# Masks added in half-height tiles beside the scores, from folded copies of the constant masks

## The chip, the cores and the metric

The kernel runs on one core of a Trainium2 chip. The metric is the device time of one launch in microseconds (us); each kernel is run several times and the median counts. The engines are TensorE (PE, with its weight loads listed apart as PEld), VectorE (DVE), ScalarE (ACT), GpSimd (POOL) and SyncE (SP), which issues all DMAs of this kernel in the order of its program.

## The reference

Two transformer layers with four kinds of attention are followed by a second block with a gated delta rule and a dilated attention. The sequence has 512 tokens and a head 64 channels. What matters here is how scores are masked; shortened:

```
# group a: causal, head width 96      # group d: causal, plus forget gates
s = einsum('bqhd,bkhd->bhqk', q_blk, k) * scale
if log_f_cum is not None:
    s = s + (cum[t] - cum[s])                       # group d only
s = where(key_pos <= qpos, s, -inf)
p = softmax(s)
# group b: sliding window of 128 keys, two key blocks, with a sink logit per head
mask = (kpos >= 0) & (kpos <= qpos) & (qpos - kpos < SWA_WINDOW)
s = where(mask, s, -inf)
# group c: each query keeps its top 128 keys by an indexer; for the first block plain causal
# second block, dilated attention, three groups: window of 2 blocks, causal, residue classes
scores = where((dist >= 0) & (dist <= n_back) & (kpos >= 0), scores, -inf)
```

## The kernel before, in words

A job is one head and one block of 128 queries: its scores against up to 512 keys, softmax, transposition of the probabilities and the product with the values. A layer has 64 jobs in 32 pairs; `layer_jobs` lists them by group in the order a, b, d, c (`JOB_ORDER`), so pairs 0 to 7 are group a, 8 to 15 group b, 16 to 23 group d, 24 to 31 group c. The dilated attention of the second block has 48 jobs in 24 pairs: 0 to 7 with the window mask, 8 to 15 causal, 16 to 23 residues. The two jobs of a pair are two heads: one has its channels in partitions 0 to 63, the other in 64 to 127 (`r` is 0 or 64). Their score products use those 64 rows of the array only, and the two stand side by side in it.

`attention` writes one program for each engine. PE's loop over p does the scores of pair p (with the mask), then, if p is odd and at least 5, the values of two earlier pairs, then, from p = 3, the transposes of pair p - 3. The scores of pair p go to four PSUM banks in turn, so they wait (`powered`) for the exponentials of pair p - 2. A mask is added by TensorE too: a bf16 identity of 128 rows times a bf16 mask of 128 rows, accumulated on the scores, one such product a job (L708). DVE then takes the row maximum (L773) and the shift (L779 or L782), ACT the exponential (L863), DVE the reciprocal (L806), POOL the scaling (L904), PE transposes (L722), ACT (in the dilated attention also DVE) copies, PE multiplies by the values (L741). On DVE steps of the key selection (L1992, L1993) stand between the pairs. Every float32 product comes as two passes, each with a weight load.

SP's program is one queue in the order of the blocks in the code. `Weights.send` (L141) issues a weight transfer when a slot of the ring is free, which it learns from the semaphore `split` that DVE's low part (L161) counts up. Before the change `attention` has no SP program; the transfers of the part before it are the last thing that SP issues until the part behind it.

Of the kernel before, what the change touches and what calls it, by code (L numbers as in the profile page):

```python
# [32 lines left out]
P = 128  # L33
S = 512
# [209 lines left out]
def opening(part, nc, sb, psum, weights, x, operand, small, a):  # L244
# [5 lines left out]
    ident_half = sb("ident_half", [P, P], BF16)  # L250
    causal_half = sb("causal_half", [P, P], BF16)
    window_half = sb("window_half", [P, 2 * P], BF16)
# [141 lines left out]
    return ((ident, ones, causal, (ident_half, causal_half, window_half), gate_forms, eps),  # L394
# [258 lines left out]

class Job:
# [5 lines left out]
    def __init__(self, scores, width, mask, scale, values, sink=None, sinks=None):  # L660
        self.scores, self.width, self.mask, self.scale = scores, width, mask, scale
        self.values, self.sink, self.sinks = values, sink, sinks
# [6 lines left out]
def attention(block, psum, jobs, stores, ident, ident_half, probs, probs_t, stats, sems, besides=None, ready={},  # L669
              freed=None, turns_ready=(), values_ready=(), held=None, fill=None):  # L670
# [9 lines left out]
     dve_own, besides_done, sink_shifted, sink_powered) = sems  # L680
# [13 lines left out]
    def _(pe):  # L694
        def scores(p):
# [201 lines left out]
    def _(pool):  # L897
# [3 lines left out]
        for j in range(n):  # L901
# [6 lines left out]
                  "dve_own besides_done sink_shifted sink_powered")  # L908
# [266 lines left out]
def layers(nc, psum, x, operand, weights, consts, vectors, plans, small, besides_last, a, first, opened, begin):  # L1175

    ident, ones, causal, (ident_half, causal_half, window), gate_forms, eps = consts
    all_gains, all_sinks, all_forget_bias = vectors
    table_rows = nc.inline_tensor(tables(), name="position_tables")
    for l, (_, n_out, n_down) in enumerate(plans):  # L1180
# [9 lines left out]
        with opened if l == 0 else ExitStack() as whole:  # L1190
            layer = first if l == 0 else whole.enter_context(part(nc))
            with ExitStack() as mix:
# [20 lines left out]
                with ExitStack() as ctx:  # L1213
                    jobs = layer_jobs(turned, values, gates, kept, causal_half, window, sinks)
# [7 lines left out]
                    probs_t = sb("probs_t", [P, 4, S], ctx)  # L1222
                    sb("kept_free", [P, T * LATENT_W + TABLE_W - 4 * S], ctx)
# [4 lines left out]
                              output.fill(stored_low, (powered, n_jobs)))  # L1228
# [768 lines left out]
def layer_jobs(turned, values, gates, chosen, causal, window, sinks):  # L1997

    jobs = []
    for group in JOB_ORDER:  # L2000
        for pair in range(2):
            for t, h in itertools.product(range(T), (2 * pair, 2 * pair + 1)):
# [4 lines left out]
                sink = both = None  # L2007
                scale = 64 ** -0.5
                if group == "a":
                    scale = 96 ** -0.5  # L2010
                    scores = [(turned[0:MLA_DIM, QA + h, q], turned[0:MLA_DIM, KA + h, 0:w])]
                    v0 = V_MLA + 64 * h
                    v = [values[:, b, v0:v0 + 64] for b in blocks]
                elif group == "b":
                    blocks = list(range(max(t - 1, 0), t + 1))
                    k0 = blocks[0] * P
                    mask = window[:, 2 * P - len(blocks) * P:2 * P]
                    sink, both = sinks[:, h:h + 1], sinks[:, 2 * pair:2 * pair + 2]
# [3 lines left out]
                elif group == "c":  # L2022
                    if t:
                        mask = chosen[:, t - 1, 0:w]
# [1445 lines left out]
```

## Time and profile before

| | us |
|---|---|
| median of 3 runs (lowest, highest) | 2065.27 (2065.0, 2066.26) |
| profiled execution, its own time | 2066.51 |
| profiled execution, span from first to last instruction | 2064.8 |

| engine | busy us | share of the span |
|---|---|---|
| PE | 1990.1 | 96% |
| PEld | 1610.8 | 78% |
| DVE | 1115.5 | 54% |
| ACT | 832.9 | 40% |
| POOL | 361.3 | 17% |

The shares are means over stages that differ. Nearly all of PE's time is in the dense products (L182 to L184); the stages that the change touches are three: the attention of layer 0 (about 170 to 255 us in the span), that of layer 1 (about 820 to 915 us) and the dilated attention (1878 to 1922 us). In these the clock of TensorE and the waits between the engines are to be read by stretches, not from the totals. In the page's line of the clock each digit is the granted share in tenths of full speed.

### The profile page before, as it was taken

The page shows a single profiled execution, that of the slowest core. Times are in us where ns is not written, and L with a number is a line of the kernel's source. Part 1 is how long each engine was busy: PE and PEld are TensorE (multiplying, and loading weights), DVE is VectorE, ACT ScalarE, POOL GpSimd, SP SyncE. Part 2 cuts the span into 40 slices and gives each one's busy share as a digit, 9 for nine tenths or more (in the row PEclk, how much of TensorE's full clock was granted, in tenths as well). Part 3 has the DMA queues.
Part 4 walks back from the last instruction along what each step waited for, and adds up shares of the span by engine and source line. Part 5 has one row for each costly group of instructions (what it writes and reads, how often), then busy time and mean ns, then how long its engine had stood idle before and what let it go on. Part 6 is the DMA issues. An engine that isn't in the chain of part 4 may idle for free. (4 is left out here: it accounts for less than half of the span.)

```text
span 2064.8 us, 27438 instructions
## 1 busy us (share of the span) xinstructions
PE 1990.1 (96%) x10488; PEld 1610.8 (78%) x10488; DVE 1115.5 (54%) x2037; ACT 832.9 (40%) x1736; POOL 361.3 (17%) x345
## 2 busy tenths in 40 slices
PE   8999999999999999999999999799999999999997
PEld 7776588888887877568888888688787987886786
DVE  5788644423434489835643543579775331525555
ACT  4445633322423244744321332453443334534532
POOL 1336700000000153740000000003031320004300
PEclk9999999999999999999999999999999999999999
DMA  6321023323333442013533433223225222341232
GB/s 192 96 79 52 1 73 110 103 92 92 99 105 79 115 107 75 12 48 107 201 136 107 168 115 110 89 77 92 83 70 146 80 71 95 93 143 42 82 123 82
DMA packets 177523, 198.27 MB, mean 96 GB/s; under 512 B 38755, under 2 KB 140786, under 8 KB 176882
## 3 DMA queue, kind: packets, MB, share of 16 engines
q1 hardware_dynamic: 177394, 196.53, 30.8%
q8 instruction: 84, 1.38, 0.3%
q14 instruction: 45, 0.37, 0.1%
HBM read 180.74 MB, written 11.55 MB: 93 GB/s over the span
## 5 line engine op out<-in xcount | busy, mean ns | idle before, releaser
L161 DVE TENSOR_TENSOR weight_pairs<-weight_ring,weight_pairs 128x1024 fp32r<-128x1024 f32 (+4 forms) x293 | 355.3, 1215 | 399.4 <-ACT weight_pairs L152 398.2
L182 PE MATMUL psum<-operand,weight_pairs 128*128 128x512 f32 x1320 | 527.3, 399 | 11.6 <-PEq L230 8.6
L184 PE MATMUL psum<-operand,weight_pairs 128*128 128x512 f32 x1320 | 517.3, 392 | 0.0
L183 PE MATMUL psum<-operand,weight_pairs 128*128 128x512 f32 x1320 | 517.2, 392 | 0.0
L152 ACT ACTIVATE weight_pairs<-weight_ring 128x1024 fp32r<-128x1024 f32 (+4 forms) x293 | 303.4, 1038 | 524.9 <-PE psum L184 510.4
L182 PEld LDWEIGHTS psum<-operand,weight_pairs 128*128 128x128 f32 x1320 | 249.3, 189 | 71.4 <-issue 19.4
L184 PEld LDWEIGHTS psum<-operand,weight_pairs 128*128 128x128 f32 x1320 | 248.8, 188 | 53.8
L183 PEld LDWEIGHTS psum<-operand,weight_pairs 128*128 128x128 f32 x1320 | 249.4, 189 | 50.8 <-issue 1.0
L904 POOL TENSOR_SCALAR probs<-probs,stats 128x128 f32<-128x128 f32 (+3 forms) x176 | 162.4, 940 | 228.6 <-DVE stats L806 227.3
L182 PE MATMUL psum<-weight_pairs,hidden 128*128 128x512 f32 x512 | 200.6, 392 | 0.0
L183 PE MATMUL psum<-weight_pairs,hidden 128*128 128x512 f32 x512 | 199.9, 391 | 0.0
L184 PE MATMUL psum<-weight_pairs,hidden 128*128 128x512 f32 x512 | 199.9, 390 | 0.0
L1351 DVE TENSOR_TENSOR mlp_work<-mlp_work 128x512 f32<-128x512 f32 x64 | 44.0, 688 | 175.3 <-ACT mlp_work L1334 175.3
L182 PE MATMUL psum<-weight_pairs,operand 128*128 128x512 f32 (+3 forms) x320 | 115.7, 362 | 5.3 <-DVE weight_pairs L161 3.7
L182 PEld LDWEIGHTS psum<-weight_pairs,hidden 128*128 128x128 f32 x512 | 96.6, 189 | 20.3 <-issue 0.2
L184 PEld LDWEIGHTS psum<-weight_pairs,hidden 128*128 128x128 f32 x512 | 96.5, 189 | 20.1
L183 PEld LDWEIGHTS psum<-weight_pairs,hidden 128*128 128x128 f32 x512 | 96.4, 188 | 20.2 <-issue 0.2
L183 PE MATMUL psum<-weight_pairs,operand 128*128 128x512 f32 (+3 forms) x320 | 112.1, 350 | 0.0
L184 PE MATMUL psum<-weight_pairs,operand 128*128 128x512 f32 (+3 forms) x320 | 112.1, 350 | 0.0
L863 ACT ACTIVATE probs<-psum,stats 128x128 f32<-128x128 f32 (+3 forms) x176 | 82.8, 482 | 28.2 <-DVE stats L779 26.1
L1334 ACT ACTIVATE mlp_work<-psum 128x512 f32<-128x512 f32 x64 | 37.6, 594 | 137.9 <-PE psum L184 137.9
L773 DVE TENSOR_REDUCE stats<-psum 128x1 f32<-128x128 f32 (+3 forms) x176 | 66.3, 418 | 29.6 <-PE psum L708 29.1
(433 smaller groups left out, 2760.8 us busy)
## 6 DMA issues: line engine op xcount, KB each, us to landing
weight_ring<-in_w_in_dram SPq DMA_DIRECT2D x100, 512.0 KB, 3.7
weight_ring<-in_w_up_dram SPq DMA_DIRECT2D x64, 512.0 KB, 3.7
weight_ring<-in_w_down_dram SPq DMA_DIRECT2D x64, 512.0 KB, 3.6
weight_ring<-in_w_out_dram SPq DMA_DIRECT2D x24, 512.0 KB, 3.5
ada_rows<-in_ada_w_dram SPq DMA_DIRECT2D x24, 512.0 KB, 4.6
spilled<-v_t SPq DMA_DIRECT2D x22, 256.0 KB, 4.3
weight_ring<-in_w_in_dram SPq DMA_DIRECT2D x20, 256.0 KB, 2.9
weight_ring<-in_w_proj_a_dram SPq DMA_DIRECT2D x8, 512.0 KB, 3.4
```

The lines of the kernel that those rows point to most:

```text
L152: act.activation(self.pairs[:, i % SPLIT_RING, 0, 0:n], self.buf[:, i % RING, 0:n], ACT.Copy).then_inc(self.rounded, 1)
L161: dve.tensor_tensor(self.pairs[:, i % SPLIT_RING, 1, 0:n], self.buf[:, i % RING, 0:n], self.pairs[:, i % SPLIT_RING, 0, 0:n].bitcast(F32), ...
L182: pe.matmul(out, lhs[0], rhs[0], start=start, stop=False)
L183: pe.matmul(out, lhs[0], rhs[1], start=False, stop=False)
L184: return pe.matmul(out, lhs[1], rhs[0], start=False, stop=stop)
L773: dve.tensor_reduce(stats[:, 4, j:j + 1], psum[:, j % SB, 0:jobs[j].width], AX_X, ALU.max).then_inc(found, 1)
L863: act.activation(probs[:, j % PB, 0:job.width], psum[:, j % SB, 0:job.width], ACT.Exp, bias=stats[:, 0, j:j + 1], scale=job.scale, accum_o ...
L904: pool.tensor_scalar(rows, rows, stats[:, 2, j:j + 1], None, ALU.mult).then_inc(normed, 1)
L1334: act.activation(self.relu[:, g % B, :], self.psum[:, g % 8, :], ACT.Relu).then_inc(self.rectified, 1)
L1351: dve.tensor_tensor(self.square[:, f % B, :], self.relu[:, f % B, :], self.relu[:, f % B, :], ALU.mult).then_inc(self.squared, 1)
```

## The change

The three bf16 constants (identity, causal mask, window mask) become one tile, `halves`. Each attention gets an SP program. It first waits for `turns_ready` (in the layers; the list is empty in the dilated attention) and then copies the constants from SBUF to SBUF into a tile `folds` of two halves: half i has rows 64i to 64i + 63 of a constant, once in partitions 0 to 63 and once in 64 to 127. That takes four copies a source: one source in a layer (4 copies of 64 x 512 in bf16), three in the dilated attention (8 copies of 64 x 128, 4 of 64 x 256). They land in memory that the stage before has freed; in the dilated attention that is the old float32 `causal`. PE waits for all of them (`masks_folded`) at the first pair that uses them: pair 8 in a layer, pair 0 in the dilated attention.

A job of groups b and d, of c in its first query block, and of the dilated groups 0 and 1 now adds its mask by two products of 64 rows each, in the same rows as its scores. Group a, the chosen masks of group c and the residue masks stay as they were. In group d the gate products (2 rows of the array) come ahead of the score products instead of behind them.

```diff
@@ attention
+    folds, sources = folded
+    by_rows = [p for p in range(len(jobs) // 2) if jobs[2 * p].mask_rows is not None]
+
+    @block.sync
+    def _(sp):
+        for sem, count_needed in turns_ready:
+            sp.wait_ge(sem, count_needed)
+        at = 0
+        for source in sources:
+            width = source.shape[1]
+            for r in (0, P // 2):
+                for i in range(2):
+                    sp.dma_start(folds[r:r + P // 2, i, at:at + width],
+                                 source[i * P // 2:(i + 1) * P // 2, :]).then_inc(masks_folded, 16)
+            at += width
@@ attention, PE, scores(p)
+            if p == by_rows[0]:
+                pe.wait_ge(masks_folded, 16 * 4 * len(sources))
+            if p in by_rows:
+                for i in range(2):
+                    for j in pair:
+                        shifted_ident, rows_of_mask = jobs[j].mask_rows[i]
+                        first = jobs[j].width - rows_of_mask.shape[1]
+                        mm = pe.matmul(psum[:, j % SB, first:jobs[j].width], shifted_ident, rows_of_mask, start=False,
+                                       stop=(i == 1))
+                        if i == 1:
+                            mm.then_inc(scored, 1)
+                return
@@ layer_jobs, group d
-                    scores = [(turned[r:r + 64, DQ + h // 2, q], turned[r:r + 64, DK + h // 2, 0:w]),
-                              (gates[32 * h:32 * h + 2, 0, q], gates[32 * h:32 * h + 2, 1, 0:w])]
+                    scores = [(gates[32 * h:32 * h + 2, 0, q], gates[32 * h:32 * h + 2, 1, 0:w]),
+                              (turned[r:r + 64, DQ + h // 2, q], turned[r:r + 64, DK + h // 2, 0:w])]
@@ new function; folds has identity at columns 0 to P, causal from P, window from 2 P
+def mask_in_halves(folds, r, at, width):
+    side = slice(r, r + P // 2)
+    return [(folds[side, i, 0:P], folds[side, i, at:at + width]) for i in range(2)]
@@ dilated attention
+                halves = mask_in_halves(folds, r, (4 * P - w, P)[g], w) if g < 2 else None
+                  folded=(folds, (ident_half[:], causal[:], window_incl[:])))
```

On PE the rows of layer 0, group b, read so before the change (`turned_qk` are scores, `ident,probs` transposes, `probs_t,values` the values):

```order
L705 MATMUL psum<-turned_qk 128x256 x2
L708 MATMUL psum<-window_half,ident_half 128x256 x2
L741 MATMUL psum<-probs_t,values 64x128 x6
L722 MATMUL psum<-ident,probs 128x128 x6
L705 MATMUL psum<-turned_qk 128x256 x2
L708 MATMUL psum<-window_half,ident_half 128x256 x2
L722 MATMUL psum<-ident,probs 128x128 x8
```

and after it:

```order
L727 MATMUL psum<-turned_qk 128x256 x2
L735 MATMUL psum<-folded_masks 128x256 x4
L775 MATMUL psum<-probs_t,values 64x128 x6
L756 MATMUL psum<-ident,probs 128x128 x6
L727 MATMUL psum<-turned_qk 128x256 x2
L735 MATMUL psum<-folded_masks 128x256 x4
L756 MATMUL psum<-ident,probs 128x128 x8
```

The places are the same; the two mask products of a pair have become four of half height.

On SP, at the way from the product stage of the second block to the dilated attention, the queue reads before:

```order
L141 DMA weight_ring<-in_w_proj_a_dram 128x4x256 x2
L141 DMA weight_ring<-in_w_in_dram 128x4x256 x6
L3194 UNCONDITIONAL_BRANCH
L3197 DMA qk<-spilled 128x6x512
L141 DMA weight_ring<-in_w_in_dram 128x4x256 x2
```

and after:

```order
L141 DMA weight_ring<-in_w_proj_a_dram 128x4x256 x2
L141 DMA weight_ring<-in_w_in_dram 128x4x256 x6
L690 UNCONDITIONAL_BRANCH
L699 DMA causal<-halves 64x128 x8
L699 DMA causal<-window_incl_half 64x256 x4
L3236 UNCONDITIONAL_BRANCH
L3239 DMA qk<-spilled 128x6x512
```

The twelve copies stand behind the last of six weight transfers and so can't be issued ahead of it. In a layer the four copies stand in the same way behind the sixth transfer of the output weights (`in_w_out`); here, of the program after, with the awaited semaphores:

```order
L141 DMA weight_ring<-in_w_out_dram 128x2x512 [waits weights_split] x6
L690 UNCONDITIONAL_BRANCH [waits front_0_copied_bk]
L699 DMA folded_masks<-halves 64x512 [waits front_0_tokens_stored]
L699 DMA folded_masks<-halves 64x512 x3
L1134 UNCONDITIONAL_BRANCH
L141 DMA weight_ring<-in_w_out_dram 128x2x512 [waits weights_split]
```

The weight transfer that used to follow the branch at once now stands behind the four copies and their wait.

## Rows read from the trace of the kernel before

**Rows 1.** The page: busy time, and the chain that ended last.
```profile
PE 1990.1 (96%) x10488; PEld 1610.8 (78%) x10488; DVE 1115.5 (54%) x2037; ACT 832.9 (40%) x1736; POOL 361.3 (17%) x345
PE 13%; ACT 1%; DVE 1%; issue 1%; ACTq 0%
```

**Rows 2.** Stretches: length, busy us per engine; clock, DMA share, GB/s.
```profile
1882.40:1889.00 6.60, 6.24 (x27) 3.58 (x28) 4.31 (x22) 4.39 (x19) 4.69 (x6) 0.50 0.00 0
...
1889.30:1900.00 10.70, 10.52 (x102) 7.05 (x100) 7.35 (x36) 7.19 (x30) 9.57 (x13) 1.00 0.01 2
190.00:200.00 10.00, 8.22 (x80) 5.41 (x78) 9.03 (x35) 7.37 (x26) 7.72 (x7) 1.00 0.15 52
```

**Rows 3.** Timeline of PE, group b of layer 0: start, length, instruction.
```profile
205.11 0.41 PE L705 MATMUL psum<-turned_qk 64*128 64x256 f32 x2
205.45 0.39 PE L708 MATMUL psum<-window_half,ident_half 128*128 128x256 bf16 x2
...
205.77 0.88 PE L741 MATMUL psum<-probs_t,values 128*64 128x128 f32 x12
206.58 0.66 PE L722 MATMUL psum<-ident,probs 128*128 128x128 f32 x4
...
207.48 0.38 PE L705 MATMUL psum<-turned_qk 64*128 64x256 f32 x2
207.80 0.39 PE L708 MATMUL psum<-window_half,ident_half 128*128 128x256 bf16 x2
208.03 0.60 PE L722 MATMUL psum<-ident,probs 128*128 128x128 f32 x4
```

**Rows 4.** The same for its weight loads.
```profile
207.27 0.19 PEld L705 LDWEIGHTS psum<-turned_qk 64*128 64x128 f32 x2
207.79 0.11 PEld L708 LDWEIGHTS psum<-window_half,ident_half 128*128 128x128 bf16 x2 [0.33 <-issue]
207.92 0.47 PEld L722 LDWEIGHTS psum<-ident,probs 128*128 128x128 f32 x4
```

**Rows 5.** Timeline of SP: last transfer before each of the three attention stages.
```profile
1875.35 0.37 SPq L141 DMA_DIRECT2D weight_ring<-in_w_in_dram  x1
...
190.15 0.37 SPq L141 DMA_DIRECT2D weight_ring<-in_w_out_dram  x1
...
836.01 0.37 SPq L141 DMA_DIRECT2D weight_ring<-in_w_out_dram  x1
```

**Rows 6.** Copies from SBUF to SBUF in the trace: timeline, and issues with us to landing.
```profile
99.44 4.98 SPq L1625 DMA_DIRECT2D turned_qk_first<-turned_qk  x8
...
turned_qk_first<-turned_qk SPq DMA_DIRECT2D x56, 64.0 KB, 2.0
```

**Rows 7.** Timeline at the start of the dilated attention, PE and DVE.
```profile
1878.70 0.29 PE L708 MATMUL psum<-window_incl_half,ident_half 128*128 128x128 bf16 x2
1881.41 0.70 PE L705 MATMUL psum<-qk,q_dilated 64*128 64x256 f32 x4 [2.42 <-DVE v_tok L2867]
...
1881.28 0.48 DVE L773 TENSOR_REDUCE stats<-psum 128x1 f32<-128x128 f32 x2
```

**Rows 8.** Timeline around the first pair of group b, layer 0, then layer 1.
```profile
192.95 0.28 PE L708 MATMUL psum<-window_half,ident_half 128*128 128x128 bf16 x2
...
193.88 0.44 PE L722 MATMUL psum<-ident,probs 128*128 128x128 f32 x2 [0.42 <-POOL probs L904]
194.78 0.70 PE L705 MATMUL psum<-turned_qk 64*128 64x256 f32 x4 [0.46 <-ACT probs L863]
...
199.73 0.66 PE L722 MATMUL psum<-ident,probs 128*128 128x128 f32 x4 [0.90 <-POOL probs L904]
...
193.93 0.47 DVE L773 TENSOR_REDUCE stats<-psum 128x1 f32<-128x128 f32 x2
...
839.20 0.28 PE L708 MATMUL psum<-window_half,ident_half 128*128 128x128 bf16 x2
```

**Rows 9.** Timeline of PE, dilated attention, clock granted at 0.50.
```profile
1884.50 1.22 PE L705 MATMUL psum<-qk,q_dilated 64*128 64x256 f32 x4
```

More of the change, by code:

```diff
@@ L651, in finish_act, with __init__ @@
             self.high(act, T - 1)
+def mask_in_halves(folds, r, at, width):
+    side = slice(r, r + P // 2)
+    return [(folds[side, i, 0:P], folds[side, i, at:at + width]) for i in range(2)]
 class Job:
-    def __init__(self, scores, width, mask, scale, values, sink=None, sinks=None):
+    def __init__(self, scores, width, mask, scale, values, sink=None, sinks=None, mask_rows=None):
+        self.mask_rows = mask_rows
         self.scores, self.width, self.mask, self.scale = scores, width, mask, scale
@@ L1213, in layers @@
                 with ExitStack() as ctx:
-                    jobs = layer_jobs(turned, values, gates, kept, causal_half, window, sinks)
+                    probs_t = sb("probs_t", [P, 4, S], ctx)
+                    folds = sb("folded_masks", [P, 2, 4 * P], ctx, BF16)
+                    jobs = layer_jobs(turned, values, gates, kept, causal_half, window, sinks, folds)
                     n_jobs = len(jobs)
@@ L1994, in select_keys, with layer_jobs @@
     return (T - 1) * per_tile, step
-def layer_jobs(turned, values, gates, chosen, causal, window, sinks):
+def layer_jobs(turned, values, gates, chosen, causal, window, sinks, folds):
     jobs = []
@@ L2017, in layer_jobs @@
                     mask = window[:, 2 * P - len(blocks) * P:2 * P]
+                    halves = mask_in_halves(folds, r, 4 * P - len(blocks) * P, len(blocks) * P)
                     sink, both = sinks[:, h:h + 1], sinks[:, 2 * pair:2 * pair + 2]
@@ L2028, in layer_jobs @@
                 else:
-                    scores = [(turned[r:r + 64, DQ + h // 2, q], turned[r:r + 64, DK + h // 2, 0:w]),
-                              (gates[32 * h:32 * h + 2, 0, q], gates[32 * h:32 * h + 2, 1, 0:w])]
+                    scores = [(gates[32 * h:32 * h + 2, 0, q], gates[32 * h:32 * h + 2, 1, 0:w]),
+                              (turned[r:r + 64, DQ + h // 2, q], turned[r:r + 64, DK + h // 2, 0:w])]
                     v0 = tok("dv") + 64 * h
                     v = [values[:, b, v0:v0 + 64] for b in blocks]
-                jobs.append(Job(scores, w - k0, mask, scale, v, sink, both))
+                jobs.append(Job(scores, w - k0, mask, scale, v, sink, both, halves))
     return jobs
@@ L3164, in dilated_attention @@
                 mask = (window_incl[:, 2 * P - w:2 * P], causal[:], residues[:])[g]
+                halves = mask_in_halves(folds, r, (4 * P - w, P)[g], w) if g < 2 else None
                 jobs.append(Job([(q[r:r + 64, c, b * P:(b + 1) * P], k[r:r + 64, c, keys])], w, mask, 64 ** -0.5,
-                                [v[:, kb, c * P + r:c * P + r + 64] for kb in blocks]))
+                                [v[:, kb, c * P + r:c * P + r + 64] for kb in blocks], mask_rows=halves))
     stores = [(permuted(y[:, c, :], c // 2), lambda bank, g=c // 2: in_order(bank, g), None)
```

32 lines of the change are left out of this document (17 added, 15 removed).

## The prediction

> **What bounds the kernel now.** I read the page first. PE is busy 96% of the span, mostly with dense products, and the chain that ended last lies on PE [rows 1]; a cost or a gain on PE's path is passed on to the end, if no wait takes it up on the way. So the question is what PE's path does in the three attention stages. I read them by stretches: in group b of layer 0 PE is busy 8.22 of 10 us and DVE 9.03, so there PE waits for the others; at the start of the dilated attention the clock is granted at 0.50 of full (1.2 GHz), and a little later it is full (2.4 GHz) and PE is busy 10.52 of 10.70 us [rows 2]. Then the timeline of PE pair by pair, and last SP's, since the change makes PE wait for copies that SP issues [rows 5].
>
> **What a mask costs now.** Passes of 128 columns in float32 follow each other at 0.11 us: four transposes take 0.60 us of which the last is 0.27 long, so 0.33 for three steps [rows 3]. A pass of 256 columns is thus 0.21 us. The second pass of the scores starts at 207.48 and has streamed by 207.70 (estimate, 207.48 + 0.21, rounded). The weights of the mask load at 207.79 [rows 4]: 0.10 us in which PE goes over from half-height tiles to the full array. The two mask products take 0.12 each, and the transposes behind them, in the same full-array form, start at 208.03 with their weights loaded under the mask, at 207.92 [rows 3, 4]. From the end of the scores to the transposes: 0.33 us. Where the values follow (odd pairs), the scores' last pass starts at 205.14 (205.11, and 0.03 more, by which the row's 0.41 is longer than the 0.38 of one pass), has streamed by 205.36, and the values begin at 205.77, to which 0.06 of open loading comes (twelve in pairs: 0.88 less 0.27 is 0.61, five steps of 0.11 are 0.55): 0.47 us, with two changes of form of 0.10 in it.
>
> **What it costs after.** The four half-height products of a pair stand two and two side by side, as the scores do: the two steps take 0.21 us together for 256 columns (a bf16 column needs half of float32's time: 0.12 with its load against 0.21). There is no change of form ahead of them, one behind.
> - Even pair, transposes follow: 0.21 + 0.10 + 0.06 (the transposes' first weights, no longer loaded under a mask; as at 206.58, where four take 0.66 instead of 0.60) = 0.37 against 0.33: 0.04 us, with the skew of the two tiles 0.05 longer.
> - Odd pair, values follow: 0.21 + 0.10 + 0.06 = 0.37 against 0.47: 0.10 us shorter.
> With masks of 128 columns both sides shrink alike and the differences stay. In group d the gate products ahead instead of behind change the order of the forms, not their number: before scores, gates, mask, after gates, scores with mask; the same sums hold.
> Count: a layer has 8 odd and 10 even pairs (b and d, and two first blocks of c), the dilated attention 6 odd and 7 even from pair 3 on. Odd: 22 x 0.10 = 2.2 us less; even: 27 x 0.05 = 1.35 more. Pairs 0 to 2 of the dilated attention lose both changes of form, at the slow clock; there PE mostly waits for ACT, so I take 0.3 less. Sum of PE's path: 1.1 us less. In group b PE waits for DVE and ACT anyway [rows 2, 8], so part of it is not seen: bounds 0 and, if every one of the 52 pairs gained 0.10, 5.2 us less. I take 1.0, nearest to the rows.
>
> A rule speaks against even this. The Trainium skill (TensorE: Matmul & The Clock Gate, Part 3, The mechanism) says that a weight load overlaps with products in flight only when it goes to another row group. The second mask product of a job goes to the row group of the first. The trace does not agree: the second weights of the scores load at 207.27, in the same 64 rows in which the first pass streams until 207.48 [rows 3, 4]. By the rule the loads would stand open; what that costs is the second rival.
>
> **The copies, the part that costs.** No such copy of bf16 constants is in the trace, but the float32 copies from SBUF to SBUF are its nearest kin: eight issues take 4.98 us, 0.62 each, and a copy lands 2.0 us after its issue [rows 6]. The other end is the 0.37 us that SP takes for a weight transfer [rows 5]. I take 0.62, since both ends of these copies are in SBUF too.
> - Dilated attention: SP's last weight transfer is issued at 1875.35 [rows 5] and can't go earlier, since it waits for a ring slot. The first copy then starts at about 1875.85, the twelfth 11 x 0.62 = 6.8 later at 1882.7, and lands at 1884.7. PE wants the masks at 1878.70 [rows 7]. Not all of these 6 us count: DVE is busy with the stage before and takes the first maximum at 1881.28, and PE's second pair waits until 1881.41 [rows 7]. After: masks at 1884.7, about 0.4 to the first maximum (two steps and the latency of a matmul at the slow clock): 1885.1. Cost 3.8 us. PE's idle time at the slow clock moves with it: I expect the clock back at full some 3.4 us later than the 1889 of before, which keeps the stretch at 1.2 GHz about as long, at no further price.
> - Layer 0: last transfer at 190.15, copies at 190.65, 191.3, 191.9 and 192.5, landed at 194.5; PE wants them at 192.95: a stall of 1.55 us. Behind the wait stand the transposes of pair 5 and all that follows. PE has waits of its own at 193.88 (0.42), 194.78 (0.46) and 199.73 (0.90, for POOL, which works off pairs scored before) [rows 8]; they take up the stall on PE. DVE's maximum of pair 8 moves from 193.93 to 194.9, and DVE is 90% busy [rows 2], so a part stays: I take 0.3.
> - Layer 1: last transfer at 836.01, landed at 840.4, wanted at 839.20 [rows 5, 8]: a stall of 1.2 us, and 0.3 stays, by the same pattern.
> The waits of SP cost nothing else: the next transfer on the queue is issued at the end of each stage. `turns_ready` is reached before the first transposes, long before pair 8. The memory traffic of the copies is small beside one weight transfer.
>
> **Sum.** 3.8 + 0.3 + 0.3 - 1.0 = 3.4, rounded to 3.5 us more. The profiled execution took 2066.5 us (span 2064.8 and 1.7 around it) and would take 2070.0; it lies 1.2 above the median, so the median goes from 2065.3 to 2068.8: 0.17% more. A measurement of this kernel can tell about 0.2%, 4.1 us, from no change, so this is no change by that bound, but near it.
>
> **Rivals.**
> - The waits are paid in full (slower). In both layers the stall is passed on by DVE, whose slack is a tenth of its time: 1.55 + 1.2 instead of 0.6, 2.1 more; and PE, idle for 6 us at the dilated attention instead of 2.4, gets one more stretch at 1.2 GHz, in which the scores of a pair take 1.22 instead of 0.70 us [rows 7, 9]: about 0.7 for two pairs with their masks. 3.5 + 2.8 = 6.3: 2071.6. It decides from the point at which PE's waits behind the stall stay as long as they were (0.42, 0.46 and 0.90 in layer 0). For it: DVE's 9.03 of 10. Against: POOL's queue is long enough that PE waits for it at 199.73 in any case.
> - The loads of the second mask products stand open, since each goes to the rows of a product in flight (slower). The mask's load at 207.79 is 0.01 ahead of its product; a float32 load shows 0.06, two tiles 0.12 [rows 3, 4]. I take the middle, 0.06 for 52 pairs, 3.1 us: 2071.9. Against it: the second weights of the scores, loaded at 207.27 under a running pass. This is the skill's rule named above, as a mechanism of this kernel.
> - The copies come cheap: issued at 0.37 each, the twelfth starts at 1879.9 and lands at 1881.9. Then the first maximum comes 1.0 instead of 3.8 later, and the stalls in the layers shrink by 0.75 each: 3.5 - 2.8 - 0.4 = 0.3: 2065.6, the same.
> - The changes of form are worth more than the count says (faster): the copies cheap, and every pair 0.10 shorter because the maximum also starts sooner: 1.4 for the waits less 5.2: 2061.5. Against it: for 256 columns the first job's mask ends no sooner than before (0.10 + 0.12 against 0.11 + 0.11), and DVE begins with it.
>
> **How the numbers follow.** Forecast 0.50, waits in full 0.22, loads open 0.05, copies cheap 0.16, faster 0.07. The forecast's own spread is 1.5 us either way (0.37 to 0.62 an issue on one side, the layers' waits on the other), so a third of it lies over 4.1 us. Slower: 0.17 + 0.19 + 0.04 = 0.40; faster 0.06, as the last rival may also end within the bound; the same 0.54. The range goes from the cheap copies, 2065.6, to the dear waits, 2071.6 and half a us for the phase of the clock: 2072.1.
>
> **What would show it.** In the profile after: twelve copies on SP 0.6 apart from 1875.8 on; PE's mask of the first dilated pair at 1884.7 and the first maximum 0.4 behind it; the mask of pair 8 at 194.5 and 840.4 with the later waits shorter; from the end of an odd pair's scores to the values 0.10 less, to an even pair's transposes 0.05 more; four mask products in two steps of 0.11. Wrong would be the forecast if the copies are issued at another pace, if the two half-height products of a step don't run side by side, or if the whole stage of a layer is over 1 us longer.

## The result, and the profile after

| | us |
|---|---|
| kernel after, median of 4 runs (lowest, highest) | 2073.89 (2072.03, 2079.86) |
| kernel before beside it, median (lowest, highest) | 2065.14 (2064.42, 2066.26) |
| ratio, with its 95% interval | 1.0042 (1.0029 to 1.0054) |
| profiled execution after, its own time / span | 2075.08 / 2073.4 |

The change costs 8.7 us, 0.42%, where 3.5 were forecast and 2072.1 was the end of the range. A second series of the same kernel gave 1.0047 (1.0030 to 1.0064).

The page of after, in the rows that answer to [rows 1] and, for SP, a new entry in the chain:

```profile
PE 1990.0 (96%) x10588; PEld 1616.6 (78%) x10592; DVE 1116.7 (54%) x2037; ACT 834.1 (40%) x1736; POOL 362.0 (17%) x345
PE 13%; ACT 1%; DVE 1%; issue 1%; SPq 0%; DMA 0%; ACTq 0%
```

PE has 100 products more in its records (104 by the program: 36 in each layer, 32 in the dilated attention) and is busy 0.1 us less, while the span is 8.6 us longer: PE's idle time grew by that much, not its busy time. SPq and DMA now stand in the chain, so the copies are on the path.

The timeline of PE in the dilated attention, which answers to [rows 7]. The number in brackets is PE's idle time just before the instruction, and what ended it:

```profile
1883.65 0.49 PE L727 MATMUL psum<-qk,q_dilated 64*128 64x128 f32 x4
1890.04 0.40 PE L735 MATMUL psum<-causal 64*128 64x128 bf16 x4 [5.90 <-DMA causal<-window_incl_half]
1890.22 1.17 PE L727 MATMUL psum<-qk,q_dilated 64*128 64x256 f32 x4
```

SP's queue ahead of it, the start and length of the issues (two weight transfers, the second at its end, then the twelve copies):

```profile
1875.28 5.81 SPq L141 DMA_DIRECT2D weight_ring<-in_w_in_dram  x2
1881.13 4.99 SPq L699 DMA_DIRECT2D causal<-halves  x8
1886.17 2.51 SPq L699 DMA_DIRECT2D causal<-window_incl_half  x4
```

and DVE's first maximum, which comes as soon as the mask is there:

```profile
1890.47 0.49 DVE L807 TENSOR_REDUCE stats<-psum 128x1 f32<-128x128 f32 x2 [3.74 <-PE psum L735]
```

All times in this kernel are 5.4 us later by then, so they are compared from the last dense product on (1877.96 before, 1883.33 after). The first maximum comes 7.14 us behind it instead of 3.32: 3.8 later, as forecast.

PE at the first pair of group b in layer 0 and in layer 1, which answers to [rows 8]:

```profile
190.95 0.49 PE L727 MATMUL psum<-turned_qk 64*128 64x128 f32 x4
193.69 0.28 PE L735 MATMUL psum<-folded_masks 64*128 64x128 bf16 x4 [2.25 <-DMA folded_masks<-halves]
193.91 0.66 PE L756 MATMUL psum<-ident,probs 128*128 128x128 f32 x4
194.49 1.23 PE L727 MATMUL psum<-turned_qk 64*128 64x256 f32 x4
195.51 0.64 PE L735 MATMUL psum<-folded_masks 64*128 64x256 bf16 x4
...
845.19 0.29 PE L735 MATMUL psum<-folded_masks 64*128 64x128 bf16 x4 [2.06 <-DMA folded_masks<-halves]
...
847.19 1.55 PE L775 MATMUL psum<-probs_t,values 128*64 128x128 f32 x12
```

Two things are to be seen. PE waits 2.25 and 2.06 us, where 1.55 and 1.2 were forecast. And behind the wait everything takes nearly twice its time: four score passes 1.23 instead of 0.70 [rows 8], twelve value passes 1.55 instead of 0.88 [rows 3]. That is TensorE at 1.2 instead of 2.4 GHz, granted so from 194.5 to 197.9 and from 846.4 to 849.8 us.

The copies themselves, by line (duration of an issue in ns, then the time to landing):

```profile
L699 SPq DMA_DIRECT2D folded_masks<-halves x8: 502/594/597, 188.8 to 842.3; - x8
L699 SPq DMA_DIRECT2D causal<-halves x8: 517/596/601, 1881.1 to 1885.5; - x8
...
DMA to landing us min/median/max: 1.8/2.5/3.6
```

The three stages by stretches, from the last dense product ahead of them to their last transposes of probabilities (so layer 0's reaches to 265 us, not 255); columns as in [rows 2]. After:

```profile
174.70:266.27 91.57, 83.08 (x687) 55.02 (x689) 58.47 (x219) 58.66 (x205) 65.70 (x64) 0.96 0.04 12
826.42:916.25 89.83, 81.50 (x688) 54.05 (x689) 58.45 (x219) 58.71 (x205) 65.71 (x64) 0.98 0.04 13
1883.33:1929.39 46.06, 37.43 (x349) 24.64 (x348) 28.60 (x146) 31.25 (x126) 32.06 (x48) 0.89 0.08 25
```

Before:

```profile
175.09:265.12 90.03, 82.49 (x653) 52.57 (x653) 58.82 (x219) 58.62 (x205) 64.65 (x64) 0.98 0.03 10
822.51:910.98 88.47, 81.12 (x654) 51.54 (x654) 58.93 (x219) 58.52 (x205) 65.70 (x64) 1.00 0.03 10
1877.96:1920.87 42.91, 37.72 (x318) 23.65 (x316) 28.44 (x146) 31.19 (x126) 32.03 (x48) 0.92 0.07 18
```

The stages explain 1.5 + 1.4 + 3.2 = 6.1 of 8.6 us. One execution is not enough for such sizes, since the stretches at 1.2 GHz fall differently each time (layer 0 had one before too). So the experiments below, each profiled once, are read by the same three stages. In the table a number in brackets is the time at 1.2 GHz inside the stage; "way" is what lies between the two attentions; the ratio is that of timed runs to the kernel before, run beside them; it can differ by up to 0.1% from the ratio of the two medians, since the runs of a kernel spread by several us.

| kernel | layer 0 | way | layer 1 | dilated | ratio (95%) |
|---|---|---|---|---|---|
| before | 90.03 (3.4) | 557.4 | 88.47 (0) | 42.91 (6.8) | |
| before, second | 88.45 (0) | 557.6 | 90.77 (6.8) | 42.72 (6.8) | |
| before, third | 90.01 (3.4) | 557.5 | 88.44 (0) | 42.85 (6.8) | |
| padded | 88.48 (0) | 560.1 | 88.47 (0) | 42.78 (6.8) | 1.0011 (1.0001 to 1.0021) |
| after | 91.57 (6.8) | 560.2 | 89.83 (3.4) | 46.07 (10.2) | 1.0042 (1.0029 to 1.0054) |
| after, second | 89.62 (3.4) | 559.2 | 89.89 (3.4) | 46.17 (10.2) | 1.0047 (1.0030 to 1.0064) |
| after, third | 92.47 (10.2) | 558.3 | 90.23 (3.4) | 46.03 (10.2) | |
| after, padded | 89.73 (3.4) | 557.8 | 92.70 (10.2) | 46.25 (10.2) | 1.0043 (1.0024 to 1.0061) |
| wait only | 88.90 (0) | 557.6 | 91.64 (6.8) | 46.72 (10.2) | 1.0026 (1.0017 to 1.0035) |
| layers late | 91.04 (6.8) | 560.2 | 90.15 (3.4) | 43.87 (10.2) | 1.0027 (1.0017 to 1.0036) |
| eight | 91.18 (6.8) | 558.3 | 88.55 (0) | 42.54 (3.4) | 1.0015 (1.0004 to 1.0026) |
| kept busy | 89.24 (0) | 557.8 | 90.82 (3.4) | 45.16 (0) | 1.0023 (1.0012 to 1.0033) |
| early | 88.02 (0) | 560.1 | 87.99 (0) | 43.94 (10.2) | 1.0007 (0.9998 to 1.0016) |
| early, no gates | 90.25 (3.4) | 559.3 | 88.63 (0) | 43.92 (10.2) | 1.0021 (1.0011 to 1.0030) |
| early, odd | 92.71 (10.2) | 557.9 | 87.92 (0) | 42.22 (6.8) | 0.9995 (0.9985 to 1.0005) |
| early, best | 87.89 (0) | 557.9 | 87.91 (0) | 42.14 (6.8) | 0.9997 (0.9988 to 1.0006) |

### The profile page after: what moved, and what is told of

It reads as the page before. It is cut to its first block and busy times, and to the rows that moved or that the text cites. A ratio compares the mean times of both kernels' runs of the same rounds, so it can differ in the third digit from the quotient of the medians.

```text
span 2073.4 us, 27662 instructions
## 1 busy us (share of the span) xinstructions
PE 1990.0 (96%) x10588; PEld 1616.6 (78%) x10592; DVE 1116.7 (54%) x2037; ACT 834.1 (40%) x1736; POOL 362.0 (17%) x345
```

## The experiments

**Again: the kernel after, unchanged.** It gives a second trace of the same kernel, and more times.

> The changed kernel as it is, timed over more rounds. Both theories: about 2072 to 2074 us, 7 to 9 us over the kernel before. If the spread of its first four runs (2072.0 to 2079.9) comes with the change, it shows again, several us wide, where the kernel before stays within 2; if it was chance, all runs lie within 2 us of 2072.

Measured: median 2078.42 of 7 runs (2072.13 to 2084.76), 1.0047. Its runs spread over 12.6 us, those of the kernel before beside them over 9.1 (2064.64 to 2073.7), not 2 as expected, and those of early, below, over 6. The time goes with the clock that was granted over the run: 2084.76 us at 0.981 and 2072.13 at 0.987 in after, 2073.7 at 0.984 and 2064.64 at 0.990 in before. The traces fit that: the three stages of the after kernel meet a varying number of stretches at 1.2 GHz.

**Early: all copies ahead of the stages.** The twelve copies go between the weight transfers of the projections, the layers' four go once in front of layer 0 into memory that later holds other masks, and `attention` has no SP program.

```diff
+                if 1 <= d <= 12:
+                    to, of, sem = early_copies[d - 1]
+                    sp.dma_start(to, of).then_inc(sem, 16)
@@ in front of layer 0
+                if begin is not None and 0 <= d - (n_dense - 6) < 4:
+                    sp.dma_start(folds[64 * r:64 * r + 64, j, :], source[64 * j:64 * j + 64, :]).then_inc(early, 16)
```

> The same masks in half-height tiles, but the folded copies are issued long ahead: once, in the front of layer 0, into memory that serves both layers, and in the projections of the second block for the dilated attention, one copy behind each weight transfer. No SP program in the attention is left. Theory A (the copies stand behind weight transfers and PE waits for them): the 2.3, 2.5 and 5.9 us waits are gone and so is the clock that fell behind them; what is left is the count of the form changes, between -1.5 and +0.5 us against the kernel before, 2064 to 2066. Theory B (half-height products or the gates' order are themselves slow or let the clock fall more often): 3 us or more over the kernel before stay, 2068 to 2071.

Measured: 2069.61 us, 1.0007. Against after this takes back 0.35%, some 7 us of the 8.7 (each of the two ratios is sure to about 0.1%): the late copies are the greater part. In the table, layer 0 and layer 1 are 88.0 and have no stretch at 1.2 GHz. That is 0.45 less than before has without one (88.44 to 88.48): what the half-height masks, together with the new place of the gates, give in a layer, where the count said 0.3.

**Wait only: the copies and the waits, but masks of full height and the gates behind.** It is the complement of early.

```diff
-            if p in by_rows:
+            if p in ():
@@ layer_jobs, group d
-                    scores = [(gates...), (turned...)]
+                    scores = [(turned...), (gates...)]
```

> The copies at their late place and PE's waits for them stay, but masks are added in full height and the gates stand behind the scores, as before the change. Theory A: as slow as the changed kernel or 1 us more, +7 to +9 us, with PE idle 2.3, 2.5 and 5.9 us at the three places. Theory B: +3 to +4 us, the waits alone, and the rest gone.

Measured: 2074.4 us, 1.0026 (5.4 us). The dilated stage is 3.9 over before (46.72 against a mean of 42.82), layer 1 met 6.8 us at 1.2 GHz, and layer 0, with none, is 88.90: 0.45 over before. Its wait is 1.51 us there, so the wait without a slow stretch costs about a third of its length.

**Early, odd: copies early, half height only in odd pairs from 5 on.** These are the pairs for which the count of the forecast promises a gain.

```diff
-    by_rows = [p for p in range(len(jobs) // 2) if jobs[2 * p].mask_rows is not None]
+    by_rows = [p for p in range(len(jobs) // 2) if jobs[2 * p].mask_rows is not None and p % 2 and p >= VALUES + 1]
```

> Copies early, and only the odd pairs from 5 on (values follow the mask) add their masks in half height; even pairs (transposes follow) in full height. The count gives 22 pairs 0.10 us shorter, 2.2 us, and no pair longer: on PE's path 1.4 us less than the run with early copies and all pairs; where PE waits for others it is not seen. Theory A: 2063.5 to 2065, 0.5 to 1.5 us under the kernel before. Theory B: between the run with early copies and the kernel before.

Measured: 2065.89 us, 0.9995. Layer 1 is 87.92, as with all pairs (87.99), so even pairs give or cost next to nothing in a layer (the gates come first in both). The dilated stage is 42.22 with 6.8 us at 1.2 GHz, and 43.94 with 10.2 when all pairs are of half height.

**Kept busy: dummy products in the wait.** The kernel after, with 40 (in the dilated attention 100) bf16 products on an unused bank in front of PE's wait.

```diff
             if p == by_rows[0]:
+                keep_busy(pe, psum[:, 7, :], ident_half, 40 if len(sources) == 1 else 100)
                 pe.wait_ge(masks_folded, 16 * 4 * len(sources))
```

> The changed kernel; only, ahead of PE's wait for the copies stand unneeded bf16 products into a free bank, 40 in a layer (2.2 us at full clock) and 100 in the dilated attention (5.5 us), which fit into the wait. The waits stay. Theory 1 (the fall of the clock behind the wait is a part of the cost): no stretch at 1.2 GHz right behind the three waits, and the stages get shorter than in the changed kernel (91.6 or 89.6, 89.8 and 46.1 us from the last dense product to the last transposes) by about 1 us in each layer and 2 us in the dilated attention. Theory 2 (the wait alone is the cost, the clock goes with it for nothing): the stages as long as in the changed kernel, within 0.4.

Measured: 2070.77 us, 1.0023: 4 us less than after, although PE does 180 products more. PE in the dilated attention:

```profile
1880.59 0.49 PE L727 MATMUL psum<-qk,q_dilated 64*128 64x128 f32 x4
1881.01 5.76 PE L96 MATMUL psum<-halves 128*128 128x128 bf16 x100
1887.83 0.29 PE L736 MATMUL psum<-causal 64*128 64x128 bf16 x4 [1.06 <-DMA causal<-window_incl_half]
1887.95 0.65 PE L727 MATMUL psum<-qk,q_dilated 64*128 64x256 f32 x4
```

The mask comes 7.2 us behind the first scores, 0.8 later than in after (6.4), yet the second scores take 0.65 instead of 1.17, and the stretch of the whole stage shows a clock of 1.00 and a length of 45.16 instead of 46.1:

```profile
1880.27:1925.43 45.16, 40.19 (x449) 28.59 (x448) 28.61 (x146) 31.09 (x126) 31.94 (x48) 1.00 0.09 26
```

Behind neither wait of the layers is there now a stretch at 1.2 GHz; the one of layer 1 is at 860.4, 3.4 us long. For the layers two places are few (5 of 14 such places had none without dummy products, as counted below); the dilated stage, with 0 where all five other executions with the twelve late copies have 10.2 us, carries the reading.

**Layers late: dilated copies early, those of the layers late.** The dilated part of early, the layers as in after.

> The changed kernel, but the twelve copies of the dilated attention are issued early, among the weight transfers of its projections; the layers keep their late copies. If the costs of the stages add: layers 89.6 to 91.6 and 89.8 us as in the changed kernel, dilated 43.9 us as with all copies early; 1.5 to 3.5 us less in all than the changed kernel, 3.5 to 5 us over the kernel before. If the prediction's step held (0.3 us a layer), it would be no slower than the run with all copies early plus 0.6 us.

Measured: 2072.16 us, 1.0027, which is 0.20% over early and so 4.1 us for the two layers' waits, and 0.15 to 0.20% under after, 3 to 4 us for the dilated wait; each of these differences is sure to about 0.15%, 3 us. In the table the layers are 91.04 and 90.15 and the dilated stage is 43.87, early's 43.94.

**Eight: eight copies in the dilated attention instead of twelve.** Identity and causal mask lie side by side in `halves` and are copied together.

```diff
-                  folded=(folds, (ident_half[:], causal[:], window_incl[:])))
+                  folded=(folds, (two_halves[:, 0:2 * P], window_incl[:])))
```

> The changed kernel, but the dilated attention folds identity and causal mask in one source, so 8 copies are issued instead of 12; the layers are unchanged. If the wait is SP's pace of 0.64 us a copy, the last lands 4 x 0.64 = 2.6 us earlier: PE waits 3.3 instead of 5.9 us and the dilated stage takes 43.5 to 44.5 instead of 46.1 us. If the wait were for the data (bytes or the time to landing, which stay), it would stay at 5 us or more and the stage at 46.

Measured: 2069.05 us, 1.0015. The wait is shorter by 2.57 us, four issues of 0.6:

```profile
1885.69 0.40 PE L735 MATMUL psum<-causal 64*128 64x128 bf16 x4 [3.33 <-DMA causal<-window_incl_half]
```

and the stage by 3.6, as only 3.4 instead of 10.2 us of it are at 1.2 GHz. If the 2.57 us count in full, the other 1.0 came with the clock; that split is argued. With 3.4 us at 1.2 GHz the stage is even no longer than before (42.82, with 6.8 us at 1.2 GHz), though PE still waits 3.33 us.

**Before again.** The kernel before, profiled for the scatter of its stages.

> The kernel before, for a second profile on this chip: the same work, so any difference to its first profile (stages of 90.0, 88.5 and 42.9 us, 1843.4 us outside of them) is what the phase of the clock and the chip make. Theory A: stages within 1.5 us of these in sum; the rest 1843 to 1846, as in the kernels with the change (1845.0 to 1847.8), so that the rest doesn't belong to the change. Rival: the rest is at 1843.4 again, and the change costs 2 us outside of its stages.

Measured: 2066.3 us. Its layers have changed places: 88.45 without a slow stretch, 90.77 with one of 6.8.

**Early, best: early odd, and half height in the first three dilated pairs too.**

```diff
+               and (p % 2 and p >= VALUES + 1 or p < TURN)]
```

> Copies early, half height in the odd pairs from 5 on (as in the run with odd pairs alone) and also in the first three pairs of the dilated attention, where no product of another form follows. Theory 'half height delays the clock' (in both profiles with all pairs in half height and early copies the slow stretch at the start of the dilated attention was 10.24 us, in the three with full height there 6.83): 10.24 us again and a dilated stage of 43.3 to 44.0 us. Rival (chance of the phase, the count of form changes decides): 6.83 us and 41.9 to 42.2 us, 0 to 0.3 less than the 42.2 of the run with odd pairs alone. Layers 87.9 us where no slow stretch falls in. Total: 2063.5 to 2066.5.

Measured: 2066.32 us, 0.9997. The dilated stage keeps its 6.8 us at 1.2 GHz and is 42.14 long: so it is not the first three pairs by which early lengthens that time to 10.2 us. Early best adds full-height masks in pair 3 and in the even pairs from 4 on. In early the stretch begins at 1884.3 us and 6.8 later PE is in pair 5, which is of half height in both kernels, so only pairs 3 and 4 can have made the difference, if the masks made it. This is the best version of the change, and it can't be told from the kernel before.

**Early, no gates: early, with the gate products behind the scores.**

> Copies early, all pairs in half height, but in group d the gates stand behind the scores as before the change, so the forms are scores, gates, mask, with one change of form more than with the gates first: 8 pairs a layer with 0.10 to 0.15 us more each. If PE binds in group d, a layer's stage without a slow stretch takes 88.8 to 89.2 us instead of 88.0; if the order of the gates is worth nothing, 88.0. Dilated stage as with early copies, 43.9 us.

Measured: 2071.27 us, 1.0021, 0.14% over early. In layer 1, where neither has a slow stretch, it is 88.63 against 87.99: 0.64 us a layer is what the gates' new place gives, in one execution of each. Two layers of it are 1.3 us, 0.06%; the other 0.08% lies within the intervals. The forecast had the order of the gates at nothing.

**After and before, third.** Each profiled once more.

> The changed kernel, for a third profile: both layers' stages 89.6 to 91.6 us with a slow stretch right behind the wait at pair 8 (seen at 4 of 4 places in its two profiles), dilated 46.1 us. If the time outside of the stages belongs to the change, the way from layer 0's attention to layer 1's is again 559 to 560 us; if it is chance it may be 557.5 as in the kernel before.

> The kernel before, third profile: layers 88.5 us plus 1.2 to 1.6 for each slow stretch that falls in, dilated 42.8 us with 6.83 us of slow clock. Between the two layers' attention 557.4 us if the way is steady in this kernel, up to 560 if its length is chance in every kernel.

Measured: 2075.71 and 2066.55 us. The dilated stage of after repeats within 0.1 us (46.07, 46.17, 46.03), its layer 0 does not: 92.47, with 10.2 us at 1.2 GHz. "A slow stretch right behind the wait" did not come true in either layer: its waits were 1.13 and 1.72 us, and its slow stretches begin at 181.5, 225.9 and 874.4 us.

**Padded: 36 more dummy products at the start of the kernel before.** The table left one thing open. The way between the attentions is 557.4 to 557.6 before, but 558.3 to 560.2 in every kernel with half-height masks in all pairs, kept busy (with 40 dummy products more by then) excepted. There SP, copying float32 blocks from SBUF to SBUF, has one issue of 1.1 to 1.9 us instead of 0.59, and at that moment a block of 16 KB is read on the instruction queue. In every trace such a block is read each 20 to 30 us here, and I took its place to follow from the number of instructions before. So 36, as many as the change adds to an attention, were added alone, where PE waits anyway.

```diff
-            keep_busy(pe, psum[:, 2, :], ident_half, 40)
+            keep_busy(pe, psum[:, 2, :], ident_half, 76)
```

> The kernel before with 36 more dummy products of TensorE (76 instead of 40) at its start, where TensorE waits 1.86 us for VectorE anyway. 36 is what the change adds to one layer's attention, so from layer 1 on TensorE's instructions have the numbers that they have in the kernel after; nothing else of the change is in it. Theory (the 1.7 us between the two attentions come from where a 16 KB block of instructions is read while the first weights of layer 1 are on their way): a block is read at 736 to 741 us, an issue of SP there takes over 1.1 us, the way between the attentions grows from 557.5 to 559.0 to 560.2 us, and the whole is 1 to 3 us over the kernel before (0.3 of it the dummies themselves). Rival (the 1.7 us are chance of the chip's phase, or come from memory that the change moved): the way stays at 557.5 and the whole within 1 us of before.

Measured: 2069.38 us, 1.0011. The way is 560.1. The block that the kernel before reads at 748.0 us is read at 738.5 here. The queues of this kernel from 736 to 742 us, with the one instruction block; then SP's copies by line (the longest 1797 ns); then PE's wait for the first weights behind them:

```profile
q1 hardware_dynamic: 942, 0.53, 38.8%
q8 instruction: 1, 0.02, 1.6%
...
L1625 SPq DMA_DIRECT2D turned_qk_first<-turned_qk x8: 512/590/1797, 735.5 to 741.1; - x8
...
755.68 0.46 PE L182 MATMUL psum<-weight_pairs,operand 128*128 128x420 f32 x1 [1.64 <-DVE weight_pairs L161]
```

The kernel before has no block there, no long issue, and waits 0.62:

```profile
q1 hardware_dynamic: 1003, 0.66, 48.1%
...
L1625 SPq DMA_DIRECT2D turned_qk_first<-turned_qk x8: 512/590/591, 735.4 to 739.8; - x8
...
755.01 0.46 PE L182 MATMUL psum<-weight_pairs,operand 128*128 128x420 f32 x1 [0.62 <-DVE weight_pairs L161]
```

But this is only 1.0 of the 2.6 us by which the way grew. The other 1.6 are there already at 672 us, ahead of the copies. In both kernels PE idles 1.85 us ahead of the dense product at 667 and 669 us, and in padded a stretch at 1.2 GHz follows, from 667.6 to 671.0; padded first, then before:

```profile
667.04 0.47 PE L182 MATMUL psum<-operand,weight_pairs 128*128 128x512 f32 x1 [1.85 <-PEq L230]
667.94 0.63 PE L182 MATMUL psum<-operand,weight_pairs 128*128 128x512 f32 x1
...
668.98 0.47 PE L182 MATMUL psum<-operand,weight_pairs 128*128 128x512 f32 x1 [1.86 <-PEq L230]
669.75 0.39 PE L182 MATMUL psum<-operand,weight_pairs 128*128 128x512 f32 x1
```

So the block has cost 1.0 us here, and that 560.1 lies in the range of its theory (559.0 to 560.2) is luck. In the other kernels with a long way no such stretch lies ahead of the copies: there PE has kept pace with before up to 742 us (within 0.15), and all of it comes at the waits behind. In the three longest (after, layers late, early: 560.1 to 560.2) a stretch at 1.2 GHz follows these waits too, at 754 to 763 us; in after's second and early without the gates, with waits as long and no such stretch, the way is 559.2 and 559.3.

**After, padded: the same 36 products in the kernel after.** Now the block is read elsewhere again.

> The kernel after with the same 36 dummy products more at its start (76 instead of 40, where TensorE waits 1.71 us). The numbers of its instructions move by 36 once more, so that the block that was read at 740 us is read some 7 us earlier. Theory of the block's place: the way between the attentions comes back from 558.3 to 560.2 to about 557.6 us, and the kernel is 1 to 2 us faster than the kernel after (ratio to before about 1.0035), although it does more. Rival (memory or chance): the way stays at 558.3 to 560.2 and the time is that of after or 0.5 us over it.

Measured: 2074.07 us, 1.0043. The way is back at 557.8, and no issue there is longer than 593 ns: the block, now read at 729.8 instead of 739.8 us, was the cause of what is gone, 0.5 to 2.4 us. The whole did not follow: in the profiled execution layer 1 met 10.2 us at 1.2 GHz (92.70), in the timed ones 1.0043 stands beside 1.0042 and 1.0047, with intervals of 0.15% either way in which 1.7 us can hide. The second half of the expectation is not confirmed.

## Why the prediction was wrong

The direction and the dilated wait were right, the layers' waits 0.7 to 0.9 us too short; the time missed by 5.1 us. Means over the rows of the table (four of before, padded among them where its way doesn't count, four of after, the padded one likewise) put the 8.7 us so (the layers' means go with the stretches that happened to fall in: without the two padded kernels they are +1.7 and +0.8):

| term | forecast | measured |
|---|---|---|
| layer 0 | 0 (stall 0.3, masks -0.3) | 90.85 - 89.24 = +1.6 |
| layer 1 | 0 (the same) | 90.66 - 89.04 = +1.6 |
| dilated attention | 3.8 - 0.5 = +3.3 | 46.13 - 42.82 = +3.3 |
| way between the attentions | 0 | 559.2 - 557.5 = +1.7 |
| not placed | 0 | 0.5 |

Of the half us that the table leaves, the traces show where some lies: between layer 1's attention and the dilated one. That stretch is 967.0 long in before and in the first two executions of after (966.9 to 967.2), but 968.6 in after's third, which has 17.1 instead of 6.8 us at 1.2 GHz between 1305 and 1336 us. No copy of the change stands there; whether the change has to do with it is not shown.

- **The odd and even pairs were right.** The timeline of after, odd pair and even pair, answers to [rows 3]:

```profile
204.78 0.70 PE L727 MATMUL psum<-turned_qk 64*128 64x256 f32 x4 [0.31 <-ACT probs L897]
205.28 0.41 PE L735 MATMUL psum<-folded_masks 64*128 64x256 bf16 x4
205.63 0.88 PE L775 MATMUL psum<-probs_t,values 128*64 128x128 f32 x12
206.43 0.66 PE L756 MATMUL psum<-ident,probs 128*128 128x128 f32 x4
207.02 0.70 PE L727 MATMUL psum<-turned_qk 64*128 64x256 f32 x4
207.56 0.38 PE L735 MATMUL psum<-folded_masks 64*128 64x256 bf16 x4
207.87 0.66 PE L756 MATMUL psum<-ident,probs 128*128 128x128 f32 x4
```

  The last score pass begins 0.38 before the end of its row (205.10 and 207.34) and streams 0.21. To the values are then 205.63 - 205.31 = 0.32, with 0.06 of open loading 0.38: 0.09 less than before, forecast 0.10. To the transposes 207.87 - 207.55 = 0.32, with 0.06 again 0.38 against 0.33: 0.05 more, as forecast. Full-height masks in wait only against half-height ones in after give 46.72 - 46.13 = 0.6 in the dilated stage, forecast 0.5. The rival of open loads has no room here: it would have made both 0.44. (The Trainium skill, TensorE: Matmul & The Clock Gate, Part 3, The mechanism, ties the overlap of loads in its list to another row group; these rows don't agree. Its first paragraph also allows a load into a background weight buffer; with that they do.)
- **The gates were taken for nothing and give 0.64 us a layer** (early, no gates, against early). The whole gain in a layer, 0.45, is hence of the size that the count gave, but not for its reason: the masks alone (88.63 against 88.46) give nothing there, 0.2 us against them if anything. I had counted changes of form only.
- **The dilated wait was right**: copies 0.64 apart, the first 0.4 behind the issue of the last weight transfer, the first maximum 3.8 later, the stage +3.9 in wait only. "The stretch at 1.2 GHz about as long, at no further price" was wrong in itself: it is 10.2 instead of 6.8 us in all executions of after. That the sum of the stage came out as forecast is thus in part luck: the wait without the longer stretch must have cost less (argued, not measured alone); kept busy, with a wait 0.8 longer and no such stretch, is 1.0 us shorter.
- **The step that failed is "a part stays: I take 0.3" for each layer**, and with it "0.3 stays, by the same pattern": the net term of a layer, forecast 0, measured +1.6. The landing was too short by the row it came from: the float32 copies landed after 2.0 us, these after 1.8 to 3.6, and the last copy of a layer, close behind a weight transfer of 512 KB, after 3.05 and 2.89; so the waits were 2.25 and 2.06. That alone would for the most part have been taken up, as I argued: eight's layer 1, with a wait of 1.48 and no slow stretch, is 88.55, 0.1 over before and 0.55 over early, and wait only's layer 0 is 0.45 over before, where I took 0.3. What I left out was TensorE's clock.
- **The clock behind the layers' waits.** A stretch of 3.4 us at 1.2 GHz began 0.5 to 1.9 us behind the awaited mask in 9 of the 14 layer stages with late copies and no dummy products (after four times two, wait only, layers late, eight); it did at that place in none of the 8 of before and padded, none of the 8 of the early kernels, and in neither of kept busy. The length of the wait parts them: it was 1.82 to 2.30 us in the nine with the stretch and 1.13 to 1.72 in the five without. So the 0.7 to 0.9 us by which the landing was taken too short may have decided it; a wait of the forecast 1.55 or 1.2 us would be among the five. (These are 14 places of this kernel, not a rule: a wait of 1.85 us at 667 us was followed by such a stretch in padded and not in before.) Each such stretch costs some 1.4 us (after's layer 0: 92.47 with three against 89.62 with one, 2.85 for two; other pairs of stages give 1.2 to 2.0). With 1.7 us at 1.2 GHz before and 5.6 after, in the mean of both layers, 3.9 more, that is 1.6 us a layer, the size of the whole difference. Of these 3.9 us 2.6 lie right behind the wait (6 stretches in 8 stages). The other 1.3 lie elsewhere in the stages (7 stretches against 4), which in 8 stages can be chance; they are not tied to the wait by any run. The rival "waits in full" had the clock, but in the dilated stage alone, and had 2.1 more for the layers by way of DVE.
- **The way between the attentions was not thought of at all.** It is the other term that was put at nothing: 1.7 us. No instruction there changes; only the number of those before. With the block elsewhere (after padded, kept busy) 0.3 of it stay.
- The last test that I named, "if the whole stage of a layer is over 1 us longer", is what came true. By one profile it could not have told, though: a layer of the unchanged kernel was 88.45 once and 90.03 another time.

Three things stay open. Why the dilated stage stays 3.4 us longer at 1.2 GHz when pairs 3 and 4 (and the later even ones) are of half height: seen in early, early without the gates and layers late against early odd and early best, with its cause not tested. How the layers' cost divides between the slow stretches behind the wait and those elsewhere. And 0.5 us of the sum, which is less than its terms are sure by.

## What to carry to other kernels

A wait of 2 us can cost 1.4 us more than what the later waits leave of it, when it stops an engine whose clock falls behind it: price it by what runs behind it at the lower clock, and try dummy products in it. Issue copies of constants long before they are wanted, off the queue that feeds the stage; where they can't go earlier, merge them, since each issue cost 0.6 us here at 64 x 128, 64 x 256 and 64 x 512. And when instructions are added, part of a small loss can lie hundreds of us away, where a block of instructions is now read beside a transfer: padding with harmless instructions tells it from the change itself, if the trace is read for where the time is lost and not only for how much. The change itself gave nothing even with its copies early (0.9995 to 1.0007).

## What the runs showed of the hardware

- A 16 KB instruction read beside SP's copies stretched one issue from 0.59 to 1.1 to 1.9 us in eight traces (after, its second and third, padded, layers late, eight, early, and early without the gates), and the next wait of PE for weights was then 1.56 to 2.68 us. Without the block it was 0.62 to 0.88 in the three executions of before and in wait only, and 1.09 to 1.16 in after padded, kept busy, early odd and early best. At 716 to 722 us the same coincidence (1458 ns in the kernel before) cost nothing.
- SP takes 0.60 us to issue a copy from SBUF to SBUF of 64 x 128 in bf16 and the same for 64 x 512 (596 and 594 ns in the rows of L699); a weight transfer of 512 KB ahead of them 0.37 [rows 5].
- A hundred dummy products in a wait of 6.8 us kept TensorE at 2.4 GHz through the whole dilated attention, where the kernel before has 6.8 us at 1.2 GHz. Its stage was still longer than before's, 45.16 against 42.82, since the wait remained.
- A wait of PE of 1.82 to 2.30 us at the first pair of group b (kernels with late copies, no dummy products in the wait) was followed by 3.4 us at 1.2 GHz in 9 of 9 places, one of 1.13 to 1.72 us in 0 of 5; ahead of a dense stage, at 667 us, one of 1.85 us was followed by it in one trace and not in another.
